# Gate and value tiles of a SwiGLU pair computed as one 2 x 2 block product with seven quarter products

## What is computed

```python
def _swiglu(x, w_gate, w_up, w_down):
    return (jax.nn.silu(x @ w_gate) * (x @ w_up)) @ w_down
```

## Time and profile before

| | |
|---|---|
| median of 3 runs | 1665.66 us (1664.6, 1665.66, 1665.85) |
| span of the profiled execution | 1663.7 us |
| PE busy | 1653.9 us, 99% of the span, 8375 matmuls |
| DVE, ACT, POOL busy | 629.7, 597.6, 704.5 us (38%, 36%, 42%) |
| chain that ended last | PE 93%, DVE 3%, ACT 2%, issue 1%, DMA 1% |
| DMA queues | 32.8% of 16 engines' time |

### The profile page before, as it was taken

The page is one execution under the profiler, slowest core; times in us unless marked ns, Lnnn a source line. Parts: engine busy times, 40 slices in busy tenths (PEclk is TensorE's granted clock), DMA queues, the critical chain, the costliest instruction groups (busy, mean ns, idle before and its releaser), DMA issues.

```text
span 1663.7 us, 20763 instructions
## 1 busy us (share of the span) xinstructions
PE 1653.9 (99%) x8375; PEld 1393.3 (84%) x8375; DVE 629.7 (38%) x1059; ACT 597.6 (36%) x911; POOL 704.5 (42%) x392
## 2 busy tenths in 40 slices
PE   9999999999999999999999999999999999999999
PEld 7888888899888888889888888898768988888888
DVE  4111121257565777656121111257763512121122
ACT  4122222247545555436221222247574322122220
POOL 4454444554572443133454444444323444344442
PEclk9999999999999999999999999999999999999999
DMA  7333243333222444123333243351113333323332
GB/s 208 91 102 92 83 117 89 101 104 111 77 64 64 127 129 144 57 77 89 91 99 101 74 117 99 92 156 42 44 32 80 86 101 93 97 83 110 99 89 77
DMA packets 296041, 157.58 MB, mean 95 GB/s; under 512 B 5265, under 2 KB 292618, under 8 KB 295946
## 3 DMA queue, kind: packets, MB, share of 16 engines
q1 hardware_dynamic: 295946, 156.26, 32.8%
HBM read 154.14 MB, written 2.10 MB: 94 GB/s over the span
## 4 chain that ended last, share of the span: by engine, by line
PE 93%; DVE 3%; ACT 2%; issue 1%; DMA 1%; POOL 0%; SPq 0%; DVEq 0%; POOLq 0%
PE bank L551 22%; PE bank L552 22%; PE bank L555 22%; PE bank L2349 2%; PE bank L2353 2%; PE bank L2350 2%; PE bank L594 2%; PE bank L595 2%; PE bank L599 2%; PE bank L2846 2%; PE bank L574 1%; PE bank L580 1%; PE bank L575 1%; PE bank L2834 1%; PE bank L2375 1%; PE bank L2594 1%
## 5 line engine op out<-in xcount | busy, mean ns | idle before, releaser
L479 POOL TENSOR_TENSOR wlo<-wraw,whi 128x1024 fp32r<-128x1024 f32 (+1 forms) x238 | 561.4, 2372 | 771.3 <-ACT whi L474 771.3
L551 PE MATMUL bank<-ahi,whi 128*128 128x512 f32 x1294 | 507.8, 392 | 0.0
L552 PE MATMUL bank<-alo,whi 128*128 128x512 f32 x1294 | 503.8, 389 | 0.0
L474 ACT CAST whi<-wraw 128x1024 fp32r<-128x1024 f32 (+1 forms) x268 | 268.0, 1025 | 232.6 <-PE bank L555 152.9
L555 PE MATMUL bank<-ahi,wlo 128*128 128x512 f32 x1294 | 320.9, 389 | 0.0
L551 PEld LDWEIGHTS bank<-ahi,whi 128*128 128x128 f32 x1294 | 243.0, 188 | 51.4 <-issue 1.2
L552 PEld LDWEIGHTS bank<-alo,whi 128*128 128x128 f32 x1294 | 242.9, 188 | 51.2 <-issue 1.4
L555 PEld LDWEIGHTS bank<-ahi,wlo 128*128 128x128 f32 x1294 | 242.9, 188 | 50.4
L1649 DVE SCALAR_TENSOR_TENSOR hval<-gate,bank 128x512 f32<-128x512 f32 x66 | 45.4, 687 | 554.4 <-PE bank L555 540.2
L1044 ACT ACTIVATE gate<-bank 128x512 f32<-128x512 f32 x66 | 39.5, 598 | 512.8 <-PE bank L555 500.6
L1658 DVE SCALAR_TENSOR_TENSOR res<-res,bank 128x512 f32<-128x512 f32 x78 | 52.7, 685 | 236.3 <-PE bank L555 163.8
(11 more groups left out here) (380 smaller groups left out, 2285.0 us busy)
## 6 DMA issues: line engine op xcount, KB each, us to landing
wraw<-in_ffn_w_gate SPq DMA_DIRECT2D x42, 512.0 KB, 3.9
wraw<-in_ffn_w_up SPq DMA_DIRECT2D x42, 512.0 KB, 3.9
wraw<-in_ffn_w_down SPq DMA_DIRECT2D x32, 512.0 KB, 3.6
wraw<-in_w_in SPq DMA_DIRECT2D x30, 512.0 KB, 4.0
wraw<-in_w_gate SPq DMA_DIRECT2D x21, 512.0 KB, 3.9
wraw<-in_w_up SPq DMA_DIRECT2D x21, 512.0 KB, 3.9
wraw<-in_w_out SPq DMA_DIRECT2D x16, 512.0 KB, 5.2
wraw<-in_w_down SPq DMA_DIRECT2D x16, 512.0 KB, 3.7
```

The costliest lines, as they stand in the source:

```text
L474: eng.copy(high_of(b)[:, 0:n], raw_of(b)[:, 0:n]).then_inc(hi_ready, 1)
L479: eng.tensor_tensor(low_of(b)[:, 0:n], raw_of(b)[:, 0:n], high_of(b)[:, 0:n], ALU.subtract).then_inc(LO[b][0], 1)
L551: eng.matmul(o, w, xhi[:, k, :], start=(k == 0), stop=False)
L552: eng.matmul(o, w, xlo[:, k, :], start=False, stop=False)
```

## The change

For 54 of the 66 pairs (all but the first four of each FFN, `FIRST_FAST = (4, 0, 0)`) the gate block and the up block are taken as a 2 x 2 block matrix: gate weights with k-tiles 0 to 3 (a1) and 4 to 7 (a2), up weights with the same halves (b1, b2). The operand x is split alike: its k halves by its token halves (256 tokens), x11, x12, x21, x22. The 2 x 2 result (gate and value, each in two token halves) comes from seven quarter products of 4 k-tiles and 256 tokens, each of 12 matmuls (4 hi x hi, 4 hi x lo, 4 lo x hi), in all 84 matmuls of 256 columns:

- sums of the weights, four for each pair on DVE (`sum_weights`): S3 = a1 + b1, S1 = b1 + b2 (in place of b1), S2 = S3 + b2, S4 = S2 + a2. S2, S3, S4 stand in `wsum`, of which there are two; the wait for its slot is for the last product of the pair two before.
- sums of the operand, four for each FFN on DVE (`turn_operand`, `turned`), with hi parts by ACT and lo parts by DVE.
- products: first a1 x11, second a2 x21, third S4 x22, fourth b2 T4, fifth S1 T1, sixth S2 T2, seventh S3 T3 (T1 to T4 are the operand sums). In PSUM several are accumulated in one bank; ACT copies partial sums between banks (256 columns each), and the seventh to SBUF (`seventh_kept`), which DVE adds to both halves of the value.
- PE's order in a pair p: sixth, seventh, fifth of p, then the first of p+1, then second, third, fourth of p. The first pair of a phase has eight products (its own first, and the first of the next pair), the last six.
- GpSimd makes the lo part of the gate block (`gate_low`), and only after S4, since it overwrites the raw gate block that S4 reads. DVE makes the lo parts of the up block (S1 and b2), of S2 and S3, and of S4.
- The hidden tile's hi part goes from DVE to ACT (`fast_hidden_hi`), its lo part from DVE to GpSimd (`fast_hidden_lo`).
- `scaled_ring` of four tiles becomes `scaled_tiles` of eight, and a DVE wait on it goes; some small buffers move.

The diff, cut to its core:

```diff
+FIRST_FAST = (4, 0, 0)
         def lo_owner(b):
+            if b in PAIR_BLOCKS:
+                return DVE if b % 2 else POOL
...
+        def wait_sum_slot(eng, p):
+            if p.n >= 2:
+                eng.wait_ge(block_done, PAIR_LIST[p.n - 2].up + 1)
...
 ACT
+            def pair_hi(p):
+                act.wait_ge(*sums.of("s1", p))
+                split_hi(act, p.up)
+                act.wait_ge(*sums.of("s2", p))
+                wait_sum_slot(act, p)
+                act.copy(p.high[:, S23], p.raw[:, S23]).then_inc(sums_hi.sem, 1)
...
+            def copy_seventh(p):
+                act.wait_ge(*products.of("seventh", p))
+                if p.n >= 2:
+                    act.wait_ge(value_done, PAIR_LIST[p.n - 2].tile + 1)
+                act.copy(seventh_kept[:, p.n % 2, :], SEVENTH_BANK).then_inc(copies.sem, 1)
...
+            def fast_pair(p, last, nxt, down):
+                split_hi(act, nxt.gate if nxt else down.base)
+                copy_sixth(p)
+                if nxt:
+                    pair_hi(nxt)
+                else:
+                    split_hi(act, down.base + 1)
+                copy_fifth(p)
+                if nxt:
+                    fourth_sum_hi(nxt)
+                    copy_first(nxt)
+                copy_seventh(p)
+                if last:
+                    fast_hidden_hi(last)
+                silu_pair(p)
+                if not nxt:
+                    split_hi(act, down.base + 2)
+                    fast_hidden_hi(p)
...
 POOL
+            def gate_low(p):
+                pool.wait_ge(*sums.of("s4", p))
+                split_lo(pool, p.gate)
...
+                    for m in range(first, PARTS[part] - 1):
+                        gate_low(pair_of(ph, m + 1))
+                        if m > first:
+                            fast_hidden_lo(pair_of(ph, m - 1))
+                    fast_hidden_lo(pair_of(ph, PARTS[part] - 2))
+                    for j in range(AHEAD):
+                        pool_weights(pool, down.base + j)
+                    fast_hidden_lo(pair_of(ph, PARTS[part] - 1))
...
 DVE
+            def sums_low(p):
+                dve.wait_ge(*sums.of("s4", p))
+                split_lo(dve, p.up)
+                dve.wait_ge(*sums_hi.of("s23", p))
+                dve.tensor_tensor(p.low[:, S23], p.raw[:, S23], p.high[:, S23], ALU.subtract).then_inc(sums_lo.sem, 1)
+                dve.wait_ge(*sums_hi.of("s4", p))
+                dve.tensor_tensor(p.low[:, S4], p.raw[:, S4], p.high[:, S4], ALU.subtract).then_inc(sums_lo.sem, 1)
+            def fast_hidden(p, scale):
...
+                link(dve.tensor_tensor(o, o, seventh_kept[:, p.n % 2:p.n % 2 + 1, :].broadcast_to([P, 2, HALF]), ALU.add))
...
+                        if j == 3:
+                            turn_operand(first_pair(ph))
+                            turned_low(first_pair(ph), (T3, T1))
+                        if j == 4:
+                            turned_low(first_pair(ph), (T2, T4))
+                        if j == 2 * first - 3:
+                            sum_weights(first_pair(ph))
+                        if j == 2 * first - 2:
+                            sums_low(first_pair(ph))
+                    for m in range(first, PARTS[part]):
+                        nxt = pair_of(ph, m + 1)
+                        if nxt:
+                            sum_weights(nxt)
+                        if m > first:
+                            fast_hidden(pair_of(ph, m - 1), scale)
+                        if nxt:
+                            sums_low(nxt)
+                    fast_hidden(pair_of(ph, PARTS[part] - 1), scale)
...
 PE
+            def product(o, w, wl, x, xl, low, first=False):
+                for k in range(HK):
+                    at = slice(k * P, (k + 1) * P)
+                    pe.matmul(o, w[:, at], x[:, k, :], start=(first and k == 0), stop=False, skip_group_check=True)
+                    pe.matmul(o, w[:, at], xl[:, k, :], start=False, stop=False, skip_group_check=True)
+                pe.wait_ge(*low)
+                for k in range(HK):
+                    i = pe.matmul(o, wl[:, k * P:(k + 1) * P], x[:, k, :], start=False, stop=(k == HK - 1), skip_group_check=True)
+                return i
...
+                    if part == 0:
+                        pe.wait_ge(*sums_lo.of(T4, first_pair(ph)))
```

More of the change, by code:

```diff
@@ L521, in pool_weights @@
                 return
-            if lo_owner(b) == POOL:
+            if lo_owner(b) == POOL and b not in PAIR_BLOCKS:
                 split_lo(eng, b)
@@ L527, in dve_weights @@
                 return
-            if lo_owner(b) == DVE:
+            if lo_owner(b) == DVE and b not in PAIR_BLOCKS:
                 split_lo(eng, b)
@@ L1872, in ffn @@
                     ph = phases[f"{name}_up{part}"]
-                    t0 = part_tile0(ph.name)
-                    for j in range(ph.n):
+                    t0, first = part_tile0(ph.name), FIRST_FAST[part]
+                    for j in range(2 * first):
                         if j % 2:
@@ L1885, in ffn @@
                     final = part == len(PARTS) - 1
+                    ahead = None if final else first_pair(phases[f"{name}_up{part + 1}"])
                     for j in range(LAST if final else KD):
@@ new lines, in multiply_second, with multiply_third @@
+            def multiply_second(p):
+                pe.wait_ge(*copies.of("first", p))
+                return product(first_bank(p), high_of(p.gate)[:, K2], low_of(p.gate)[:, K2], *operand_quarter(1, 0),
+                               LO[p.gate])
+            def multiply_third(p):
+                pe.wait_ge(*copies.of("fifth", p))
+                pe.wait_ge(*sums_hi.of("s4", p))
+                return product(second_bank(p), p.high[:, S4], p.low[:, S4], *operand_quarter(1, 1),
+                               sums_lo.of("s4", p))
@@ new lines, in multiply_fourth, with multiply_fifth @@
+            def multiply_fourth(p):
+                pe.wait_ge(*copies.of("fifth", p))
+                product(value_bank(p)[:, COLS[0]], high_of(p.up)[:, K2], low_of(p.up)[:, K2], *operand_sum(T4),
+                        LO[p.up]).then_inc(block_done, 1)
+            def multiply_fifth(p):
+                pe.wait_ge(*copies.of("sixth", p))
+                wait_hi(pe, p.up)
+                product(second_bank(p), high_of(p.up)[:, K1], low_of(p.up)[:, K1], *operand_sum(T1),
+                        LO[p.up]).then_inc(products.sem, 1)
@@ L2462, in ffn @@
+                    for m in range(first, PARTS[part]):
+                        fast_pair(pair_of(ph, m), m == first, pair_of(ph, m + 1))
                     if once and part == 0:
```

263 lines of the change are left out of this document (240 added, 23 removed).

## The result

The changed kernel takes 1669.97 us (median of 13 runs, 1663.77 to 1675.85), the kernel before 1665.4 (13 runs, 1664.0 to 1666.08); the ratio is 1.0027, 95% interval 1.0015 to 1.0039. It is slower by about a quarter of a per cent, 4.6 us between the medians; 2.1 had been forecast. The spans of the two profiled executions stand 5.0 us apart, 1668.7 against 1663.7.

A forecast was written before the change was run, and what follows sets the result against it. PE, busy 99% of the span, was taken as the bound. Middle pairs -29.9, first pairs +3.9, phase ends +4.1, operand sums +9.6 and clock +14.4 sum to +2.1: 1667.8 us from 1665.66, range 1651 to 1682.

The forecast's parts named there:

- The price of a narrow matmul: PE's 256-column matmuls: 117.8 ns behind 512-column work, 113.3 to 113.8 behind a true wait; half or 4% more than half.
- Rival 4: Narrow matmuls at 117.8 ns throughout, clock as charged: +6.3 us, 1674; chance 0.13.
- Middle pairs: 36 pairs set by the loop through DVE sums, GpSimd's gate lo part and PE: 10.05 us against 10.88, -29.9 us.
- Phase ends: Nine up-phase ends: PE waits 3.5 or 2.4 us for lo parts of down blocks 0 and 1; +4.1 us net.
- Operand sums: DVE late for the opening pairs of three FFNs: 1.6, 4.0 and 4.0 us, +9.6; bounds 0 and 15.
- The clock: After each of nine phase-end stalls the granted clock falls, 1.6 us lost each: +14.4 us; bounds 0 and 17.6.
- Sum: Whole kernel: -29.9 + 3.9 + 4.1 + 9.6 + 14.4 = +2.1 us, giving 1667.8.
- Rival 1: Phase-end stalls come but the clock stays: 1653.4 us; chance 0.17.
- Rival 2: DVE and GpSimd block each other and DVE bounds the middle pair, 0.6 us more each: +21.6, 1689; chance 0.13.
- Rival 3: Stalls at phase ends are shorter, or operand sums cost nothing: -10 to -20 us, 1648 to 1658; chance 0.17.
- Rival 5: The loop isn't the bound, all products run at 9.5 us a pair, no stalls: 1592 us; chance under 0.01.

The follow-up runs named there:

- e7: e4 with five plain pairs instead of four at the start of each FFN, products in their old order, so no opening pair has a wait: 1615.73 us.
- e1: The changed kernel with GpSimd making the lo parts of down blocks 0 and 1 ahead of the last hidden tile but one's lo part: 1633.33 us.
- e2: The changed kernel with PE doing 14 (or 9) unread 512-column matmuls between an up phase's last product and the down phase: 1662.18 us.
- e3: e1 with five plain pairs instead of four at the start of each FFN: 1621.43 us.
- e4: e1 with GpSimd making the gate block's lo part in two halves, after S3 and after S4: 1615.16 us.
- e5: e4 with the sixth product before the seventh in each phase's opening pair, so PE waits once for ACT's copy: 1604.7 us.
- e6: e5 with five plain pairs instead of four at the start of each FFN: 1602.3 us, ratio 0.9623 to the kernel before.

## Why the prediction was right, step by step

- **The price of a narrow matmul**: right. Opening pairs without a wait took 11.31 us, as worked out; turns and last pairs came out by 113.3 ns (8.16 for 72 matmuls). That the slower figure stays where no wait comes was read off and is what e7 shows; that the faster one follows a wait held for all 36 middle pairs in the profiled run of the changed kernel. This was in part luck: in e1, e2 and e3, with the same loop, a third of the waits in middle pairs were followed by the slow cadence (35 of 105). Rival 4 (117.8 throughout) didn't come.
- **Middle pairs**: the loop is the bound (e4), 10.11 us where 10.05 was worked out. 36 x (10.11 - 10.88) = -27.7 against -29.9. The difference lies behind PE's wait: the lo third of four matmuls starts at 181.03 and the next product at 181.61, 0.58 us for what four steps of 113.3 ns would do in 0.45; the handovers were a little shorter than I had them. PE's wait is the 0.5 of the prediction: after 180.45 the next matmul was due at 180.56 and came at 181.03. The view gives 0.30 because it counts from the modelled end of the matmul before.
- **Phase ends**: right in place, cause and size. 8.16 + 3.55 = 11.71 us for 11.7, and 8.16 + 2.47 = 10.63 for 10.6; e1 shows the cause. In the first FFN's part 0 other work of PE stands between and the wait is 2.8, so +3.7 instead of +4.1. What the prediction didn't ask is whether GpSimd has time earlier: it has 6.9 us, and e1 uses it.
- **Operand sums**: the total was near (2.5, 4.4 and 2.0, in all 8.9, where 1.6, 4.0 and 4.0 had been worked out) by luck: two steps of it were wrong and nearly made up for one another. GpSimd's 4.76 us at 788.42, for which DVE was made to give way, are lo parts of blocks that are pair blocks now; they go, and S4 was ready at 801.66, not at 805.1. Against that GpSimd's lo part, which I had at 2.4, took 3.4 there, since DVE's L517 had started on the port 0.04 us before it:

```profile
801.70 1.22 DVE L517 TENSOR_TENSOR wlo<-wraw,whi 128x1024 fp32r<-128x1024 f32 x1
802.84 3.37 DVE L2088 TENSOR_TENSOR wsum_lo<-wsum,wsum_hi 128x1024 fp32r<-128x1024 f32 x1
...
801.74 3.39 POOL L517 TENSOR_TENSOR wlo<-wraw,whi 128x1024 fp32r<-128x1024 f32 x1 [7.87 <-DVE wsum L2082]
811.32 3.38 POOL L517 TENSOR_TENSOR wlo<-wraw,whi 128x1024 fp32r<-128x1024 f32 x1 [6.19 <-DVE wsum L2082]
...
1353.90 2.40 POOL L517 TENSOR_TENSOR wlo<-wraw,whi 128x1024 fp32r<-128x1024 f32 x1 [6.19 <-DVE wsum L2082]
...
1354.30 3.08 DVE L517 TENSOR_TENSOR wlo<-wraw,whi 128x1024 fp32r<-128x1024 f32 x1 [0.48 <-ACT whi L512]
```

  And the sums of the *second* pair, which come behind these and another hidden tile, were not in my working at all: their gate lo part ended at 814.70 and PE waited 2.48 us for it, where 0.4 stood for all that follows the first. In the first FFN it is this second wait alone that came, in the third the first alone. The Trainium skill, "SBUF — State Buffer", section "SBUF: two separate sides", has the rule that whichever of the two engines starts first keeps the shared port for its whole instruction; the rows agree, 3.39 for 2.40 and 3.37 for 1.22. In the third FFN GpSimd's second lo part began 0.40 us ahead of DVE's and took its 2.40, and DVE's took 3.08 for 1.22: the order decides who waits.
- **The clock**: right, and the term that made the sign. Nine falls of 1.6 us were charged, 14.4; ten came, inside the seven to eleven that the prediction allowed. Behind 512-column work a stretch of 3.41 us holds 8 matmuls at 0.426 us where 15 fit at 0.227, which is 1.6 again, less where it begins before PE is back, as at 324.40. The first 45 steps behind the nine stalls took 12.5 us more in all than 45 x 0.2267 each, and the two stretches behind openings are charged with 1.6 each: 15.7. That each stall is followed by one fall was wrong in detail: three phase ends had none, two had two, two openings had one each. e2 shows the mechanism at the phase ends (no idle PE, no fall), e1 that it goes with the stall. How many falls a run gets changes its time by some 10 us, so a median this near to the forecast is in part luck.
- **Sum**: -27.7 + 3.9 + 3.7 + 8.9 + 15.7, and +0.6 for the wait at L632 (1.9 before, 2.5 now), which I hadn't listed: +5.1, against the 5.0 of the spans.
- **Rival 1** (no fall): fell. **Rival 2** (the port becomes the bound): the handovers are there, DVE had 1.1 us to spare in a turn and 0.56 in e4, where the contention is greater. **Rival 3** (shorter stalls): fell. **Rival 5** held only that the order excludes it, and e4 shows that the order can be changed for half of the block.

## What to carry to other kernels

When an algorithm takes matmuls away, look for the loop that returns to PE through other engines, and for the place where the new order puts an old, easily hidden step behind a fresh result: here the change's 48 us for the matmuls (36 middle, nine last, nine opening pairs) were all spent at nine phase ends, three openings and the clock, and moving one step on an engine that had idle time gave 36 us back. An operation that waits for the last of several inputs can often be cut where its first consumer needs only a part of it. And a stall of PE should be charged with what the clock takes behind it, not with its own length alone: here 15.7 us beside 35.6 us of waits.

## What the runs showed of the hardware

- Back-to-back matmuls of 256 columns ran at one of two cadences, 117.8 or 113.3 ns (9.89 against 9.52 us for 84), and in middle pairs changed between them only at a wait of PE. A wait of 0.45 us (0.79 in two) put into each opening pair was followed by the faster one for the rest of the phase in all nine (e5), and made this kernel 10.5 us faster. In e1, e2 and e3 waits were also followed by the slower one, 35 of 105.
- The same stall isn't always followed by a fall of the clock: 2.3 us at 956.9 and 1496.8 and 2.8 us at 97.6 had none, 2.3 us at 204.1 had one, 3.4 us at 1072.2 two. In e4 a wait of 2.6 us at L633 was followed by none, where the 1.9 us at the same place was followed by one in the kernel before, in e3 and in e6, and by none in e2 and e7. e7, which has no longer stall than that one behind its start, repeats to 0.3 us; the changed kernel spreads over 12 us, and its granted clock with it.
